# Retention's last product from split operands: three passes of high and low parts in place of one fp32 matmul

## The reference

```python
def retention(q, k, v):                    # 4 heads, dk = 256, dv = 512, chunks of 128 tokens
    def step(state, inp):
        qc, kc, vc = inp
        scores = jnp.einsum('bhnd,bhmd->bhnm', qc, kc) * decay_in
        o = (jnp.einsum('bhnm,bhmv->bhnv', scores, vc)
             + jnp.einsum('bhnd,bhdv->bhnv', qc, state) * q_dec[None, :, :, None])
        state = (state * chunk_dec[None, :, None, None]
                 + jnp.einsum('bhmd,bhmv->bhdv', kc * k_dec[None, :, :, None], vc))
        return state, o

ro = retention(rq, rk, rv)                 # rv: columns of  proj = rms_norm(x, norm_mix) @ w_in
ro = rms_norm(ro, ret_norm.reshape(RET_HEADS, RET_V_DIM)).reshape(B, S, RET_V_W)
a_ret = (ro * jax.nn.silu(rg)) @ w_br
```

## Time and profile before

| what | value |
|---|---|
| median of 3 runs | 1156.4 us (1155.43 to 1156.7) |
| the profiled execution | 1156.29 us |
| its span, first to last instruction | 1154.5 us |
| TensorE busy | 1149.2 us of the span |
| VectorE busy | 750.8 us |
| ScalarE busy | 625.3 us |
| mean granted clock of TensorE | 1.00 |

### The profile page before, as it was taken

The page is one execution under the profiler, slowest core; times in us unless marked ns, Lnnn a source line. Parts: engine busy times, 40 slices in busy tenths (PEclk is TensorE's granted clock), DMA queues, the critical chain, the costliest instruction groups (busy, mean ns, idle before and its releaser), DMA issues.

```text
span 1154.5 us, 15810 instructions
## 1 busy us (share of the span) xinstructions
PE 1149.2 (100%) x5699; PEld 957.8 (83%) x5699; DVE 750.8 (65%) x1006; ACT 625.3 (54%) x959; POOL 67.5 (6%) x79
## 2 busy tenths in 40 slices
PE   9999999999999999999999999999999999999998
PEld 6788888888888888888898887788888888888887
DVE  5977666556684666546679779555745667566564
ACT  6687554444568555435456455556654455354444
POOL 3001100000000100000040042000000000000000
PEclk9999999999999999999999999999999999999999
DMA  9644565665554556565566555444655555665542
GB/s 307 189 143 124 173 196 186 187 192 185 165 164 163 155 194 198 182 189 193 171 194 212 168 164 163 132 113 128 181 189 188 181 177 182 188 193 187 194 151 106
DMA packets 95444, 203.48 MB, mean 176 GB/s; under 512 B 7901, under 2 KB 11637, under 8 KB 95392
## 3 DMA queue, kind: packets, MB, share of 16 engines
q1 hardware_dynamic: 94048, 199.68, 55.0%
q0 software_dynamic: 1184, 3.04, 0.9%
q10 hardware_dynamic: 160, 0.07, 0.0%
HBM read 201.70 MB, written 1.06 MB: 176 GB/s over the span
## 4 chain that ended last, share of the span: by engine, by line
PE 97%; DVE 1%; ACT 1%; DMA 0%; POOL 0%; issue 0%; ACTq 0%
PE pair L736 18%; PE pair L738 17%; PE pair L737 17%; PE pair L856 8%; PE turn_ps L856 8%; PE turn_ps L858 4%; PE pair L858 4%; PE score L736 4%; PE score L738 4%; PE score L737 4%; PE turn_ps L767 3%; PE score L949 0%; PE score L1199 0%; PE score L1200 0%; DMA raw<-in_w_in 0%; PE score L999 0%
## 5 line engine op out<-in xcount | busy, mean ns | idle before, releaser
L1793 DVE TENSOR_TENSOR w_lo<-raw,w_hi 128x1024 fp32r<-128x1024 f32 (+2 forms) x380 | 455.7, 1224 | 183.6 <-ACT w_hi L1329 182.4
L1329 ACT ACTIVATE w_hi<-raw 128x1024 fp32r<-128x1024 f32 (+2 forms) x380 | 389.7, 1049 | 233.5 <-DMA raw<-in_mlp_w 76.4
L736 PE MATMUL pair<-w_hi,a_both 128*128 128x512 f32 (+3 forms) x528 | 211.6, 401 | 0.2 <-ACT lat_sb L1374 0.2
L738 PE MATMUL pair<-w_hi,a_both 128*128 128x512 f32 (+3 forms) x528 | 203.7, 386 | 0.0
L737 PE MATMUL pair<-w_lo,a_both 128*128 128x512 f32 (+3 forms) x528 | 202.9, 384 | 0.0
L856 PE MATMUL pair<-a_both,w_hi 128*128 128x512 f32 x384 | 141.4, 395 | 0.0
L856 PE MATMUL turn_ps<-a_both,w_hi 128*128 128x512 f32 x384 | 141.1, 395 | 0.0
L738 PEld LDWEIGHTS pair<-w_hi,a_both 128*128 128x128 f32 x528 | 99.1, 188 | 20.2
L736 PEld LDWEIGHTS pair<-w_hi,a_both 128*128 128x128 f32 x528 | 99.3, 188 | 19.2 <-issue 0.7
L737 PEld LDWEIGHTS pair<-w_lo,a_both 128*128 128x128 f32 x528 | 99.4, 188 | 18.2 <-issue 1.0
L858 PE MATMUL turn_ps<-a_both,w_lo 128*128 128x256 f32 x384 | 107.6, 280 | 0.0
(11 more groups left out here) (403 smaller groups left out, 1675.6 us busy)
## 6 DMA issues: line engine op xcount, KB each, us to landing
raw<-in_mlp_w SPq DMA_DIRECT2D x128, 512.0 KB, 4.0
raw<-in_w_in SPq DMA_DIRECT2D x64, 512.0 KB, 3.7
raw<-in_w_up SPq DMA_DIRECT2D x32, 512.0 KB, 4.5
raw<-in_w_down SPq DMA_DIRECT2D x32, 512.0 KB, 4.3
raw<-in_attn_w_in SPq DMA_DIRECT2D x24, 512.0 KB, 5.8
raw<-in_mlstm_w_in SPq DMA_DIRECT2D x24, 512.0 KB, 3.7
raw<-in_w_br SPq DMA_DIRECT2D x16, 512.0 KB, 4.1
raw<-in_attn_w_out SPq DMA_DIRECT2D x8, 512.0 KB, 3.2
```

Source lines behind the costliest of these rows:

```text
L736: pe.matmul(o, hi, whi, start=start, stop=False)
L738: return pe.matmul(o, lo, whi, start=False, stop=stop)
L1329: act.activation(w_hi[:, k % RING, 0:n], raw[:, k % RING, 0:n], ACT.Copy).then_inc(hi_ready, 1)
L1793: dve.tensor_tensor(w_lo[:, k % RING, 0:n], raw[:, k % RING, 0:n], w_hi[:, k % RING, 0:n], ALU.subtract).then_inc(lo_ready, 1)
```

## The change

The values and the decayed scores are written as high and low parts, and `ret_value` calls `product` three times instead of issuing three fp32 matmuls.

- ACT empties `rv{n}` into `v_hi` instead of `work`, and gains `scores_hi(h)`: one 128x384 copy of `ret_s` to `s_hi`.
- DVE gains `scores_lo(h)`, one 128x384 subtraction, and `value_lo(n)`, two instructions 128x512 that read the accumulator of `rv{n}`, scale it and subtract `v_hi`. These two count as emptying the group: `dve` of `rv{n}` goes from 0 to 2.
- TensorE waits for `s_lo` and for the low values before `ret_value(h)`, and in `open_pair` also for DVE's emptying of `rv{n}`.
- `v_hi` lies in the memory of `work` and `v_lo` in that of `gate_raw`, both of which are free or taken over at that point; `s_hi` and `s_lo` hold one head each.

```diff
@@ -169,7 +169,7 @@
     for n in range(4):
         group(f"ukv{n}", w["w_ukv_2"], n * HALF, HALF, "latkv", KV_LORA // P, 2, 0)
     for n in range(4):
-        group(f"rv{n}", win, at[2] + n * HALF, HALF, "x5", DC, 2, 0)
+        group(f"rv{n}", win, at[2] + n * HALF, HALF, "x5", DC, 2, 2)
         if n:
             group(f"ret{n - 1}", None, 0, HALF, None, 0, 2, 2)
     group("rg0", win, at[3], HALF, "x5", DC, 2, 0)
@@ -408,7 +408,11 @@
         lq_sb = sb("lq_sb", [TT, MLA_H, MLA_QK], scope=ph)
         ret = sb("ret", [TT, RET_H * RET_V], scope=ph)
         ret_s = sb("ret_s", [RET_H, SCORE], scope=ph)
+        with ExitStack() as part:
+            v_hi = sb("v_hi", [2, TT, HALF], F32R, scope=part)
         work = sb("work", [2, TT, HALF], scope=ph)
+        s_hi = sb("s_hi", [SCORE], F32R, scope=ph)
+        s_lo = sb("s_lo", [SCORE], F32R, scope=ph)
         mask = sb("mask", [SCORE], scope=ph)
         rope_gain = sb("rope_gain", [2, ROPE], scope=ph)
         lat_ss = sb("lat_ss", [2, TT], scope=ph)
@@ -446,6 +450,8 @@
             lk_n = sb("lk_n", [MLA_H, S], scope=ph)
             lk_t = sb("lk_t", [MLA_H, S], scope=ph)
             l_work = sb("l_work", [2048], scope=ph)
+            with ExitStack() as part:
+                v_lo = sb("v_lo", [2, TT, HALF], F32R, scope=part)
             gate_raw = sb("gate_raw", [2, TT, HALF], scope=ph)
         lk_flat = lk_n[:, :, :].rearrange("p h s -> p (h s)")
         rot = l_work[:, 0:TT * MLA_H * ROPE].rearrange("p (t h d) -> p t h d", t=TT, h=MLA_H)
@@ -548,6 +554,8 @@
         ret_scored = sem("ret_scored")
         ret_decayed = sem("ret_decayed")
         ret_out = sem("ret_out")
+        ret_s_hi = sem("ret_s_hi")
+        ret_s_lo = sem("ret_s_lo")
         ret_norm = sem("ret_norm")
         l_squares = sem("l_squares")
         l_sq = sem("l_sq")
@@ -1168,12 +1176,16 @@
 
             def ret_value(h):
                 ps = open_pair(f"ret{h}")
-                pe.wait_ge(ret_decayed, h + 1)
-                pe.wait_ge(group_act, groups[f"rv{h}"]["act_end"])
-                v = work[:, h % 2, :, :]
-                pe.matmul(ps[:, 0, :], ret_s[:, h, 0:P], v[:, 0, :], start=True, stop=True)
-                pe.matmul(ps[:, 1, :], ret_s[:, h, P:S], v[:, 0, :], start=True, stop=False)
-                pe.matmul(ps[:, 1, :], ret_s[:, h, TALL], v[:, 1, :], start=False, stop=True).then_inc(ret_out, 1)
+                pe.wait_ge(ret_s_lo, h + 1)
+                pe.wait_ge(group_dve, groups[f"rv{h}"]["dve_end"])
+                hi, lo = v_hi[:, h % 2, :, :], v_lo[:, h % 2, :, :]
+
+                def add(tt, cols, key_tile, start, stop):
+                    return product(ps[:, tt, :], s_hi[:, cols], s_lo[:, cols], hi[:, key_tile, :], lo[:, key_tile, :],
+                                   start, stop)
+                add(0, slice(0, P), 0, True, True)
+                add(1, slice(P, S), 0, True, False)
+                add(1, TALL, 1, False, True).then_inc(ret_out, 1)
 
             def mla_turn(which, part, b):
 
@@ -1691,7 +1703,14 @@
                     act.wait_ge(ret_out, n - 1)
                 else:
                     wait_turn(act, "rk1b")
-                empty(f"rv{n}", [work[:, n % 2, tt, :] for tt in range(TT)], scales=row_norm(5))
+                empty(f"rv{n}", [v_hi[:, n % 2, tt, :] for tt in range(TT)], scales=row_norm(5))
+
+            def scores_hi(h):
+
+                act.wait_ge(ret_decayed, h + 1)
+                if h:
+                    act.wait_ge(ret_out, h)
+                act.activation(s_hi[:, :], ret_s[:, h, :], ACT.Copy).then_inc(ret_s_hi, 1)
 
             def empty_gate(n, func=ACT.Copy):
 
@@ -1705,17 +1724,21 @@
                 act.activation(gates[n], gates[n], ACT.Silu).then_inc(gate_silu, 1)
 
             dense("rv0")
+            scores_hi(0)
             empty_value(0)
             dense("rv1")
             empty_value(1)
             ret_squares(0)
+            scores_hi(1)
 
             dense("rv2", {n: (lambda n=n: mla_copy("mq", n)) for n in range(4)})
             empty_value(2)
             ret_squares(1)
+            scores_hi(2)
             dense("rv3", {n: (lambda n=n: mla_copy("mk", n)) for n in range(4)})
             empty_value(3)
             ret_squares(2)
+            scores_hi(3)
             dense("rg0")
             empty_gate(0)
             ret_squares(3)
@@ -2265,6 +2288,22 @@
                 dve.scalar_tensor_tensor(ret_s[:, h, :], score[:, h % 2, 0:SCORE], RET_QK ** -0.5, ret_s[:, h, :],
                                          ALU.mult, ALU.mult).then_inc(ret_decayed, 1)
 
+            def scores_lo(h):
+
+                dve.wait_ge(ret_s_hi, h + 1)
+                dve.tensor_tensor(s_lo[:, :], ret_s[:, h, :], s_hi[:, :], ALU.subtract).then_inc(ret_s_lo, 1)
+
+            def value_lo(n):
+
+                if n >= 2:
+                    dve.wait_ge(ret_out, n - 1)
+                ps = group_ps(f"rv{n}")
+                for tt in range(TT):
+                    dve.wait_ge(group_act, groups[f"rv{n}"]["act_end"] - TT + tt + 1)
+                    dve.scalar_tensor_tensor(v_lo[:, n % 2, tt, :], ps[:, tt, :], rstd[:, 5, tt:tt + 1],
+                                             v_hi[:, n % 2, tt, :].bitcast(F32), ALU.mult, ALU.subtract)\
+                        .then_inc(group_dve, 1)
+
             def ret_value(h):
                 dve.wait_ge(group_act, groups[f"ret{h}"]["act_end"])
                 for tt in range(TT):
@@ -2388,13 +2427,21 @@
                 dense(f"ukv{n}")
                 ret_decay(n)
             dense("rv0", {0: mla_sums_q, 3: mla_sums_k})
+            scores_lo(0)
+            value_lo(0)
             dense("rv1", {0: lambda: mla_q(0), 1: lambda: mla_q(1), 2: mla_k})
+            value_lo(1)
             ret_value(0)
+            scores_lo(1)
             dense("rv2", {n: (lambda n=n: mla_rot_copy("mq", n - 2)) for n in (2, 3)})
             mla_k_rot()
+            value_lo(2)
             ret_value(1)
+            scores_lo(2)
             dense("rv3")
+            value_lo(3)
             ret_value(2)
+            scores_lo(3)
             dense("rg0", {n: (lambda n=n: mla_rot_copy("mk", n)) for n in range(2)})
             ret_value(3)
             dense("rg1", {n: (lambda n=n: mla_slot(n)) for n in range(4)})
```

## The result

| kernel | median | runs | ratio to the kernel before |
|---|---|---|---|
| before | 1156.4 us (1155.43 to 1156.7) | 5 | |
| changed | 1169.14 us (1168.61 to 1169.82) | 5 | 1.011, 95% interval 1.010 to 1.0121 |

The change makes the kernel slower by 12.7 us. The forecast was 1168.7 us, with a range from 1165.9 to 1170.9.

The account below looks back on a forecast made before the run. TensorE, busy 1149.2 of 1154.5 us, was taken to bound the kernel. Waits and head 3's saving made 10.2 us, the slow clock 2.2: 12.4 on 1156.29 gave 1168.7 us, range 1165.9 to 1170.9.

Parts of the forecast that it names:

- wait before `rv2`: TensorE stands still 9.6 us after `ret_value(0)` until VectorE's `value_lo(1)` ends at 715.29 us; +9.4 us.
- slow clock: After the long idleness before `rv2`, TensorE resumes at the 1.2 GHz pace for a while; +2.2 us.
- wait before `rv3`: `value_lo(2)` stands behind the last transposed copy and `mla_k_rot` in VectorE's list, delaying `rv3`; +0.95 us.
- wait before `rg0`: VectorE's second `v_lo` adds 0.75 us after ScalarE empties `rv3`, delaying `rg0`; +0.35 us.
- head 3: After `ret_value(3)`, `rg1` waits only for ScalarE's emptying of `rg0`, done in time: full saving, -0.47 us.
- The deciding row: VectorE finishes its `rv1` list and starts copying `ret0` only at 712.08 us, a lag of 8.5 us behind TensorE.
- The product: In `ret_value`, nine passes of 0.233 us replace three fp32 matmuls of 0.86 us, saving 0.47 us a head, 1.9 for four.
- the saving of head 0 is lost in the wait: At `ret_value(0)`, the shorter product ends at 705.65 us, but TensorE then waits 9.6 us, so its saving disappears.
- the first rival: TensorE waits as forecast but resumes at full pace after the idleness: 1166.5 us, chance 0.13.
- the longer stall: Something in VectorE's gapless stretch gets slower or waits, or the slow clock costs more: 1171.2 us, chance 0.08.
- a wait elsewhere: A TensorE wait outside those forecast before `rv2`, `rv3` and `rg0` would show the prediction wrong; no size given.
- third rival: `value_lo(1)` done by 705.65 us, other waits covered: 1154.4 us, chance 0.03; with only the two small waits, +0.4 us.

Follow-up runs that it names:

- The first experiment: Changed kernel with the two low-value instructions of `rv1` moved ahead of `mla_q(1)` in VectorE's list; 1159.08 us, ratio 1.0025.
- the second experiment: Changed kernel with its high and low parts and all waits kept, but `ret_value` again as three fp32 matmuls; 1169.31 us, ratio 1.0112.
- The first mended version: Changed kernel with `value_lo(1)` ahead of `mla_q(1)`, attention transposes and copies one unit later, `value_lo(2)` ahead of the transposed copies; 1156.82 us, ratio 1.0005.

## Why the prediction was right

Its steps, before and after. The waits and head 3 are measured from the start of `ret_value(h)` to the second pass of the group behind it, the clock from the second pass of `rv2` to the start of `ret_value(1)`:

| step | forecast | measured | from |
|---|---|---|---|
| wait before `rv2` | +9.4 us | +9.7 | 706.19 - 703.39 = 2.80, then 715.51 - 702.99 = 12.52 |
| slow clock | +2.2 | +2.4 within `rv2` | 719.62 - 706.19 = 13.43, then 731.31 - 715.51 = 15.80 |
| wait before `rv3` | +0.95 | +1.1 | 722.43 - 719.62 = 2.81, then 735.21 - 731.31 = 3.90 |
| wait before `rg0` | +0.35 | +0.6 | 737.82 - 735.00 = 2.82, then 751.16 - 747.70 = 3.46 |
| head 3 | -0.47 | -0.5 | 752.28 - 749.47 = 2.81, then 765.15 - 762.85 = 2.30 |

These sum to 13.3 us. The stage began 0.4 us earlier in the profile after than in that before (702.99 against 703.39), which makes 12.9, against 12.8 us between the spans. That difference arises at the start of the program, where the first dense pass came at 7.54 instead of 7.98 us. It is no effect of the change: other versions with the change have 7.65 to 8.12 us there.

**The deciding row.** The forecast rested on VectorE's copies of `ret0` at 712.08 us, 8.5 us behind TensorE. With 1.80 us inserted ahead of them, `v_lo` was forecast to end at 715.29 us and ended at 714.85; with the earlier start of the stage that is 0.04 us off. The first experiment shows that the place in the list, and not the amount of work, was the cause.

**The product.** 0.233 us a pass held, in a trace (702.99 to 704.84 is eight steps of 0.23) and in time (2.07 us for four heads against the forecast 1.9). The trace of the second experiment agrees with the step that said the saving of head 0 is lost in the wait (`rv2` starts at 714.96 and 714.95 us).

**The clock.** It fell to 0.50, with passes 0.427 us apart, and filling the wait gave 2.6 us back, against a forecast 2.2 and bounds from 0 to 3.4. Of the first rival, the stall without the clock, this leaves nothing, and nothing shows the second, the longer stall. The forecast took the slow stretch from the start of the program; that its size fits is in part luck, since it differs between executions: 3.9, 4.0 and 5.9 us in three profiles. The Trainium skill, "TensorE: Matmul & The Clock Gate", "Part 1: The HAM clock gate", says that the slow state is the default and activity lifts it. The traces agree with that rule: the granted clock was 0.50 at the restart after 5.0, 8.9 and 9.7 us without matmuls.

**What was mis-sized.** The wait before `rg0`: I let VectorE's first `v_lo` run beside ScalarE's second emptying and counted only 0.75 us behind it. In the trace `v_lo` begins some 0.15 us after ScalarE's first half and takes 1.41 us from there. The terms were too small by 0.3 us for `rv2`, 0.15 for `rv3`, 0.3 for `rg0` and 0.2 for the clock. Most of the 0.3 for `rv2` is the clock again: the second pass came 0.56 us after the first (715.51 - 714.95), at the slow pace, where I had 0.34. Luck took back 0.4 of all this, the earlier start. So the median came out 0.4 us above the forecast.

**What was expected of the profile and not there.** The waits don't stand under `v_lo`'s name. Whoever had looked for VectorE in the list of waits would have found "issue" and ScalarE. The end of `v_lo` beside TensorE's restart, 0.1 us apart, is what tells. And I had called a wait elsewhere a sign of being wrong: there is one, 0.8 us for `in_x` at the start of the program. It doesn't make the time, since the first dense pass came earlier than before.

**What the third rival left out.** For the case that only the two small waits are left it had +0.4 us. The first experiment comes nearest to that case and measured +2.8 us. The two small waits are those of the changed kernel (1.33 us before `rv3`, 0.85 us before `rg0`), but two things were missing from the sum: the saving of head 0 is lost even there, since `rv2` still waits 0.25 us, and moving `value_lo(1)` forward makes the rotary embedding late, 1.62 us at the transposes. The first mended version shows the same kind of miss in my own expectation: without these waits VectorE's lag reaches `rv3`. VectorE must be followed beyond the first place where it bites.

## What to carry to other kernels

An engine that is off the critical path may be many microseconds behind without a row that shows it as a wait; before giving it an instruction that the critical engine waits for, read at what time it reaches that point of its list, and put the instruction ahead of work that nobody needs yet. Price a wait of the matrix engine with the time at the slow clock behind it, here 2.6 us on 9.7 and 1.8 us on 5.0. When a stall is removed, follow the late engine on to the next place where somebody waits for it.

## What the runs showed of the hardware that I had not expected

- After a wait of 5.0 us the clock was slow: the passes were 0.43 us apart for 3.9 us. After 8.9 us of waiting it was 4.0 us, after 9.7 us 5.9 us. Waits of 0.25, 1.28 and 1.66 us before the same kind of pass left it at 0.23 us a pass.
- Matmuls on a tile of zeros kept the clock up: with 36 of them in the wait, the granted clock was 1.00 and the passes 0.23 us apart from the first on.
- At the start of the program the granted clock can't be read off the profile's rows. In the kernel before it reads 1.00 for the first 5 us (the number after the five engines), while the nine matmuls there are 0.44 us apart, nearly twice the 0.23 us of later ones; the spacing shows the slow clock, the row doesn't:

```profile
0.00:5.00 5.00, 3.81 (x9) 1.19 (x9) 0.27 (x1) 1.28 (x1) 1.91 (x9) 1.00 0.54 187
```

- VectorE's scaled subtraction with a factor for each row (`v_lo`, 128x512) took 0.744 us, a plain one of that shape (`h_lo<-hid,h_hi`) 0.686 us; two of the scaled ones in a sequence take 1.40. The accumulator isn't the reason: a multiplication with a factor for each row that reads no accumulator (`ret<-ret,ret_r,work`) takes 0.744 us as well, and an instruction of the same name with a constant in its place (`hid<-up_sum`) 0.684 us.
